# Two decoder layers in one program block, with the first norm's 1/rms applied after the u products

## The chip, the cores and the metric

The kernel runs on one core of a Trainium2 chip. The metric is the device time of one launch in microseconds (us), the median of the runs shown; lower is better. All engine names are those of the profile: PE multiplies matrices, DVE (VectorE), ACT (ScalarE) and POOL (GpSimd) work on elements, SP issues most transfers.

## What is computed

One inference step of a two-layer decoder on 544 tokens (512 of a new sequence, 32 of eight running ones), all in fp32, d_model 1024. What the change touches is the head of a layer and its end:

```python
def layer_step(x, ...):
    h = rmsnorm(x, norm1_g[l])              # x * rsqrt(mean(x*x) + eps) * g
    u, v, o, ig, fg, q, kv, ng, ga, gb = split_cols(h @ w_in[l])
    h_a = mlstm_branch(u, v, o, ig, fg, ...) # causal conv of u, chunked matrix memory
    h_b = nsa(q, kv, gates)                  # compressed + selected + window attention
    merged = sigmoid(ga) * (h_a @ w_branch_a[l]) + sigmoid(gb) * (h_b @ w_branch_b[l])
    x = x + merged @ w_out[l]
    g_ff, u_ff = split(rmsnorm(x, norm2_g[l]) @ w_ffn_up[l])
    x = x + (silu(g_ff) * u_ff) @ w_ffn_down[l]
# two layers, then y = rmsnorm(x, final_norm_g)
```

The caches, states and new rows of both layers are outputs too.

## The kernel before

Activations lie transposed: xT holds x as 8 chunks of 128 channels by 544 tokens; hT (the normed x) has the same shape in the slab. A product with a 128-column piece of a weight is one "group": for each of 8 chunks, two matmuls of 128x128 by 128x272 into a pair of PSUM banks. Four pairs rotate; GROUPS gives the order and the pair of each of the 147 groups of a layer. Weights come as 131 units of 512 KB per layer (UNITS), through a ring of 8 places that SP fills as places come free.

The program is three blocks. The first loads x (8 transfers), the constants and the page table, and sums the squares of x: ACT squares a chunk, DVE adds it to acc. Then a hardware loop over the layers (`nc.Fori(0, DEPTH)`) holds one block in which each engine runs its own list; at its end all layer semaphores are cleared and all engines meet (`nc.all_engine_barrier()`). The last block makes the final norm: a matmul of ones by acc, a root on ACT, a reciprocal on DVE, 8 multiplications and 8 transfers out.

Within a layer, in PE's order: group n1 (ones times acc, which sums the squares over partitions, L799); the four u groups (product, L789); five tm groups (v and the token-major part of kv, L850 and L855); the gates; o; the mLSTM core; q and k; the attention; the branches, out, and the feed-forward in two halves, each ended by eight dn groups (L829). After a dn group DVE adds it to xT (L1924), ACT squares the chunk (L1261) and DVE adds the square to acc (L1548), so that the next layer's n1 finds its sum.

The head of a layer: ACT takes the root of n1 (root, L1276), DVE the reciprocal of all 544 columns (L1567), then makes the 8 chunks of hT by one operation each, `(xT * n1g) * rstd` (L1569), and PE's u groups wait for them chunk by chunk (h_ready). ACT copies each u group into upad with three copies (L1282 to L1285), DVE convolves it (L1581 to L1585), and ACT makes a rounded copy xh of hT (L1289).

SP starts a layer with the small weights' first 40 columns (L645, scales: n1g and others), then unit 0, the rest of the small weights (L654) and the further units (L650). POOL starts a layer with a 2 MB copy of the old window (L668) and four 512 KB loads of the memory state (L672, c0).

In the mLSTM core PE's sample_state(h, a) (L943) adds to the states of the running sequences; each waits until DVE's add_state (L1693) has emptied the bank of the one before it. numerators(h) (L968) waits for DVE's quotients(h-1) (L1674 to L1679). sample_rows on DVE (L1716 to L1723) finishes the 32 sample tokens.

Of the kernel before, what the change touches and what calls it, by code (L numbers as in the profile page):

```python
# [36 lines left out]
P = 128  # L37
# [41 lines left out]
RING = 8  # L79
# [4 lines left out]
GROUPS = ([("n1", 0)] + [("u", m) for m in range(4)] + [("tm", i) for i in range(TT + 1)] + [("if", 0)]  # L84
# [17 lines left out]
QSPLIT, LSPLIT = 4, 12  # L102

# [64 lines left out]
def build_step(nc, xT_in, W_in, small_in, const_in, c0_in, pages_in, table_in, win_in, cwin_in,  # L168
               y_out, fm_out, raw_out, knew_out, tm_out, u_out, pC_out, pn_out, m_out, sC_out, oldwin_out):
    with ExitStack() as ctx:  # L170
        def sb(name, shape, dt=F32):
            return ctx.enter_context(nc.sbuf_tensor(name, shape, dt))

        def sem(name):
            s = ctx.enter_context(nc.semaphore(name))
            layer_sems.append(s)
            return s

        layer_sems = []
# [187 lines left out]
        unit_landed = [sem(f"unit_landed{s}") for s in range(RING)]  # L367
# [4 lines left out]
        page_landed = [sem(f"page_landed{i}") for i in range(4)]  # L372
        raw_ready = sem("raw_ready")
        page_arranged = sem("page_arranged")
        sel_landed = sem("sel_landed")
        win_landed = sem("win_landed")
        c0_landed = [sem(f"c0_landed{h}") for h in range(MH)]
        stored = sem("stored")
        cstored = sem("cstored")
# [15 lines left out]
        u_stored = sem("u_stored")  # L395
        mix_stored = sem("mix_stored")
        raw_stored = sem("raw_stored")
        nsa_stored = sem("nsa_stored")
# [51 lines left out]
        dve_step = sem("dve_step")  # L450
        act_step = sem("act_step")
# [10 lines left out]
        with nc.Block() as block:  # L462
            @block.sync
            def _(sp):
                for k in range(KC):
                    sp.dma_start(xT[:, k, :], xT_in[:, k, :]).then_inc(x_landed[k], 16)
                sp.dma_start(const[:, :], const_in).then_inc(const_landed, 16)
                sp.dma_start(table[:, :], table_in).then_inc(table_landed, 16)

            @block.scalar  # L470
            def _(act):
                for k in range(KC):
                    act.wait_ge(x_landed[k], 16)
                    if k >= 3:
                        act.wait_ge(start_added, k - 2)
                    act.activation(acc[:, :] if k == 0 else sq[:, k % 2, :], xT[:, k, :], ACT.Square).then_inc(start_squared, 1)

            @block.vector
            def _(dve):
                dve.memset(ones[:, :], 1.0)  # L480
                dve.memset(eps[:, :], EPS)
                for k in range(1, KC):
                    dve.wait_ge(start_squared, k + 1)
                    if k >= 2:
                        dve.wait_ge(start_added, k - 1)
                    dve.tensor_tensor(acc[:, :], acc[:, :], sq[:, k % 2, :], ALU.add).then_inc(start_added, 1)
                dve.wait_ge(start_added, KC - 1)

# [97 lines left out]
        def read_out(eng, key):  # L590

            q = GROUP[key]
            eng.wait_ge(pair_free[q % 4], q // 4 + 1)

        def unit_used(eng, n):

            kind, m = UNITS[n]
            if kind == "tm" and m < KC - 1:
                eng.wait_ge(tm_used, m + 1)
            elif kind == "w1":  # L600
                eng.wait_ge(w1_used, m + 1)
            elif UNITS[n] in SPLIT:
                eng.wait_ge(wl_ready, SPLIT[UNITS[n]] + 1)
            else:
                group = ("tm", TT) if kind == "tm" else (kind, m)
                eng.wait_ge(pair_done, GROUP[group] + 1)

        def split_used(eng, n):

            kind, m = SPLITS[n]  # L610
            if kind != "dn":
                eng.wait_ge(pair_done, GROUP[("b", m) if kind == "ab" else SPLITS[n]] + 1)
            else:
                f, u = divmod(m, NFH)
                if u < NFH - 1:
                    eng.wait_ge(dn_used, f * (NFH - 1) + u + 1)
                else:
                    eng.wait_ge(pair_done, GROUP[("dn", f * KC + KC - 1)] + 1)
# [21 lines left out]
        with nc.Fori(0, DEPTH) as layer:  # L640
            with nc.Block() as block:
                @block.sync
                def _(sp):
                    parameters = small_in[bass.ds(layer, 1)].rearrange("l p n -> (l p) n")
                    sp.dma_start(small[:, 0:SMALL_FIRST], parameters[:, 0:SMALL_FIRST]).then_inc(scales_landed, 16)  # L645

                    def unit(n):
                        if n >= RING:
                            unit_used(sp, n - RING)
                        sp.dma_start(ring[:, n % RING, :],  # L650
                                     W_in[bass.ds(layer, 1), n].rearrange("l p n -> (l p) n")).then_inc(unit_landed[n % RING], 16)

                    unit(0)
                    sp.dma_start(small[:, SMALL_FIRST:SMALL_W], parameters[:, SMALL_FIRST:SMALL_W]).then_inc(small_landed, 16)  # L654
                    for n in range(1, len(UNITS)):
                        unit(n)

                    sp.wait_ge(stored, 32)
                    sp.wait_ge(u_stored, 16)
                    sp.wait_ge(mix_stored, 32)  # L660
                    sp.wait_ge(cstored, 16 * MH)
# [1533 lines left out]
```

## Time and profile before

| | |
|---|---|
| three timed runs | 2114.97, 2116.30, 2118.91 us; median 2116.3 us |
| profiled execution | 2117.96 us, its span 2115.6 us |
| PE busy | 2011.2 us, 95% |
| DVE, ACT, POOL busy | 43%, 32%, 4% |
| mean granted PE clock | 0.95 of 2.4 GHz |

The span runs from the first to the last instruction of the core; 2.4 us of the execution's time lie around it. The profiled execution is 1.7 us above the median. A timeline row gives the start, the length, the engine, the line and the operation; what stands in brackets is the engine's idle time just before, and what ended it.

### The profile page before, as it was taken

What the parts mean: (1) busy time and instruction counts of PE and PEld (TensorE: products, weight loads), DVE (VectorE), ACT (ScalarE), POOL (GpSimd) and SP (SyncE); (2) the same over time, 40 slices, a digit from 0 to 9 for tenths busy, and PEclk for the clock granted to TensorE, in tenths of its full rate; (3) what the DMA queues carried; (4) which work ended last, traced back from release to release, by engine and by line L of the source; (5) the groups of instructions that cost most, each with busy time, mean ns of one, the idle gap of its engine ahead of it and who ended that gap; (6) DMA issues with size and microseconds to landing.
All of it is one profiled execution on the core that took longest, in us unless ns stands there. A gap on an engine that the chain in (4) does not pass through costs nothing. (4 is left out here: it accounts for less than half of the span.)

```text
span 2115.6 us, 34303 instructions
## 1 busy us (share of the span) xinstructions
PE 2011.2 (95%) x14138; PEld 1774.4 (84%) x14138; DVE 910.4 (43%) x1594; ACT 667.4 (32%) x1261; POOL 84.2 (4%) x136
## 2 busy tenths in 40 slices
PE   6999999999999999999779999999999999999995
PEld 5586955589999999999756869555899999999995
DVE  4145545633345442444232355565233554424433
ACT  2443256632233221222114322556322332212221
POOL 0001120000000000000000021200000000000000
PEclk9999979979999999999889899799799999999997
DMA  7211450012222222221042023400122222222211
GB/s 273 74 69 52 135 171 1 1 60 90 90 82 89 90 90 82 90 90 51 34 183 110 21 84 121 151 1 11 61 90 91 90 81 91 90 90 83 88 41 43
DMA packets 48114, 176.33 MB, mean 83 GB/s; under 512 B 6506, under 2 KB 6538, under 8 KB 47506
## 3 DMA queue, kind: packets, MB, share of 16 engines
q1 hardware_dynamic: 40754, 144.81, 19.9%
q0 software_dynamic: 7200, 29.27, 4.1%
q8 instruction: 114, 1.87, 0.4%
q14 instruction: 46, 0.38, 0.1%
HBM read 163.47 MB, written 14.71 MB: 84 GB/s over the span
## 5 line engine op out<-in xcount | busy, mean ns | idle before, releaser
L829 PE MATMUL ps<-xh,late_w 128*128 128x272 f32 x3840 | 645.4, 289 | 1.8 <-issue 1.8
L829 PEld LDWEIGHTS ps<-xh,late_w 128*128 128x128 f32 x3840 | 544.9, 190 | 2.5 <-issue 2.3
L1557 DVE TENSOR_TENSOR late_w<-ring,late_w 128x1024 fp32r<-128x1024 f32 x196 | 240.2, 1226 | 653.8 <-ACT late_w L1272 653.8
L1272 ACT CAST late_w<-ring 128x1024 fp32r<-128x1024 f32 x196 | 205.3, 1047 | 727.0 <-PE ps L829 727.0
L829 PE MATMUL ps<-xl,late_w 128*128 128x272 f32 x1920 | 397.6, 289 | 0.0
L829 PEld LDWEIGHTS ps<-xl,late_w 128*128 128x128 f32 x1920 | 303.5, 190 | 0.0
L829 PE MATMUL ps<-ah,late_w 128*128 128x272 f32 x1408 | 234.7, 288 | 0.0
L829 PEld LDWEIGHTS ps<-ah,late_w 128*128 128x128 f32 x1408 | 198.7, 188 | 0.0
L1425 ACT ACTIVATE slab<-ps,stat 128x31 f32<-128x31 f32 (+5 forms) x204 | 84.3, 449 | 118.0 <-DVE stat L1840 118.0
L829 PE MATMUL ps<-mh,late_w 128*128 128x272 f32 x576 | 98.9, 289 | 0.0
L1075 PE MATMUL ps<-slab 64*128 64x512 f32 (+2 forms) x192 | 93.6, 615 | 0.0
L1112 PE MATMUL ps<-slab,vkv 128*64 128x256 f32 x320 | 90.9, 429 | 0.0
L1112 PEld LDWEIGHTS ps<-slab,vkv 128*64 128x64 f32 x320 | 44.0, 151 | 50.8 <-issue 34.3
L829 PEld LDWEIGHTS ps<-mh,late_w 128*128 128x128 f32 x576 | 82.3, 188 | 0.1
L789 PE MATMUL ps<-slab,ring 128*128 128x272 f32 x256 | 64.1, 416 | 18.8 <-DVE slab L1569 18.8
L829 PE MATMUL ps<-al_first,late_w 128*128 128x272 f32 x384 | 79.3, 288 | 0.0
L789 PEld LDWEIGHTS ps<-slab,ring 128*128 128x128 f32 x256 | 51.9, 204 | 31.7 <-issue 20.3
L1435 ACT ACTIVATE slab<-slab,stat 128x128 f32<-128x128 f32 (+4 forms) x140 | 69.0, 555 | 10.7 <-DVE stat L1863 10.4
L1094 PEld LDWEIGHTS ps<-const,slab 128*128 128x128 f32 (+1 forms) x384 | 43.6, 145 | 34.3 <-issue 23.3
L1094 PE MATMUL ps<-const,slab 128*128 128x128 f32 (+1 forms) x384 | 61.1, 300 | 6.0 <-ACT slab L1435 6.0
L829 PE MATMUL ps<-al_rest,late_w 128*128 128x272 f32 x320 | 66.2, 288 | 0.0
L829 PE MATMUL ps<-ml,late_w 128*128 128x272 f32 x320 | 66.1, 288 | 0.0
(324 smaller groups left out, 2688.1 us busy)
## 6 DMA issues: line engine op xcount, KB each, us to landing
ring<-in_W SPq DMA_DIRECT2D x262, 512.0 KB, 3.2
slab<-in_pages POOLq DMA_DIRECT2D x64, 128.0 KB, 2.5
slab<-in_c POOLq DMA_DIRECT2D x8, 512.0 KB, 18.3
out_sC<-slab POOLq DMA_DIRECT2D x8, 512.0 KB, 3.0
slab<-in_win POOLq DMA_DIRECT2D x2, 2048.0 KB, 8.8
out_oldwin<-in_cwin POOLq DMA_DIRECT2D x2, 2016.0 KB, 13.7
xT<-in_xT SPq DMA_DIRECT2D x8, 272.0 KB, 4.3
out_y<-slab SPq DMA_DIRECT2D x8, 272.0 KB, 2.1
```

The lines of the kernel that those rows point to most:

```text
L789: mm = pe.matmul(out[:, a, :], w[:, k, :], src[:, k, a * NHALF:(a + 1) * NHALF], start=(k == 0), stop=(k == kcs - 1))
L829: mm = pe.matmul(out[:, a, :], w[:, k * P:(k + 1) * P], x[:, a * NHALF:(a + 1) * NHALF], start=start, stop=stop)
L1075: mm = pe.matmul(out[:, r], qrT[hd, r0 + r, i * P:(i + 1) * P], kT[hd, brs[0] - 1:brs[-1], 0:(i + 1) * P], start=True, stop=True)
L1094: mm = pe.transpose(ps[0:rows, 5 + x % 2, at:at + P], part, ident)
L1112: mm = pe.matmul(out, vkv[:, j, (br - 1) * P + g * HD:(br - 1) * P + (g + 1) * HD], PT[:, x % 2, 2 * c * P:2 * (c + 1) * P], start=(br == ...
L1272: act.copy(hi, ring[:, u % RING, :]).then_inc(wh_ready, 1)
L1425: ins = act.activation(prob(k)[:, r, :], score(k)[:, r, :], ACT.Exp, bias=stat[:, k % 3, r:r + 1], accum_out=stat[:, 3 + k % 3, r:r + 1] i ...
L1435: ins = act.activation(prob(k)[:, r, :], prob(k)[:, r, :], ACT.Copy, scale=stat[:, 8 + k % 3, r:r + 1])
L1557: dve.tensor_tensor(lo, ring[:, u % RING, :], hi.bitcast(F32), ALU.subtract).then_inc(wl_ready, 1)
```

## The change

Both layers are written out one after the other in one block; the loop, the clearing of semaphores, the barrier and the separate first and last blocks are gone. Semaphores that count per layer go on counting: `on(s, value)` adds the layer's number times the total per layer (TIMES). Semaphores of stores and loads get one copy per layer. Weight units are numbered through both layers (g = 131 * layer + n), so SP goes on filling the ring into the next layer.

The head of a layer is new. DVE makes `hT[k] = xT[k] * n1g` chunk by chunk (gained), at the start of the program as each chunk of x lands, in the second layer behind each of the last eight dn additions. The u groups work on this and wait for it (xg_ready); group n1 comes behind u 0. When the reciprocal is there, DVE takes each u group out of PSUM with a multiplication by rstd (evac_u, three operations, in place of ACT's three copies), and multiplies each chunk of hT by rstd in place once group u 3 has read it (u_read); the tm groups wait for that (h_ready).

```diff
-GROUPS = ([("n1", 0)] + [("u", m) for m in range(4)] + [("tm", i) for i in range(TT + 1)] + [("if", 0)]
+GROUPS = ([("u", 0), ("n1", 0)] + [("u", m) for m in range(1, 4)] + [("tm", i) for i in range(TT + 1)] + [("if", 0)]
...
+                scales(0)
+                for k in range(KC):
+                    sp.dma_start(xT[:, k, :], xT_in[:, k, :]).then_inc(x_landed[k], 16)
+                    if k in (1, 5):
+                        unit(k // 4)
+                parameters(0)
+                for g in range(2, RING):
+                    unit(g)
+                sp.dma_start(const[:, :], const_in).then_inc(const_landed, 16)
+                sp.dma_start(table[:, :], table_in).then_inc(table_landed, 16)
+                for g in range(RING, DEPTH * len(UNITS)):
+                    layer, n = divmod(g, len(UNITS))
+                    if layer + 1 < DEPTH and UNITS[n] == ("fg", NFH):
+                        sp.wait_ge(*on(xl_ready, 2 * KC, layer))
+                        scales(layer + 1)
+                        parameters(layer + 1)
+                    unit(g)
...
-                    norm_sum(("n1", 0), None)
-                        fm("u", m, ready=(h_ready, 0))
+                        product(("u", m), ("u", m), hT, KC, (xg_ready, 0), u_read if m == 3 else None).then_inc(pair_done, 1)
+                        if m == 0:
+                            norm_sum(("n1", 0), None)
...
+                            if i == 0:
+                                pe.wait_ge(*on(h_ready, k + 1))
...
-                    sample_state(1, 1)
                     numerators(3)
+                    sample_state(1, 1)
...
+                def gained(k):
+                    return dve.tensor_scalar(hT[:, k, :], xT[:, k, :], sml("n1g")[:, k:k + 1], None, ALU.mult)
+                for k in range(KC):
+                    dve.wait_ge(x_landed[k], 16)
+                    gained(k).then_inc(xg_ready, 1)
+                    if k >= 1:
+                        dve.wait_ge(start_squared, k + 1)
+                        if k >= 2:
+                            dve.wait_ge(start_added, k - 1)
+                        dve.tensor_tensor(acc[:, :], acc[:, :], sq[:, k % 2, :], ALU.add).then_inc(start_added, 1)
...
+                    for m in range(3):
+                        evac_u(m)
                     for k in range(KC):
-                        dve.scalar_tensor_tensor(out=hT[:, k, :], in0=xT[:, k, :], scalar=sml("n1g")[:, k:k + 1], in1=rstd[:, :],
-                                                 op0=ALU.mult, op1=ALU.mult).then_inc(h_ready, 1)
+                        if k < KC - 1:
+                            dve.wait_ge(*on(u_read, k + 1))
+                        else:
+                            dve.wait_ge(*on(pair_done, GROUP[("u", 3)] + 1))
+                        dve.tensor_tensor(hT[:, k, :], hT[:, k, :], rstd[:, :], ALU.mult).then_inc(h_ready, 1)
+                    evac_u(3)
...
-                    sample_rows()
                     weighted_scores(3)
                     add_state(1, 0)
                     quotients(2)
-                    add_state(1, 1)
+                    sample_rows()
                     split_low(QSPLIT)
...
                     quotients(3)
+                    add_state(1, 1)
...
+                            if name == "dn" and m >= KC and layer + 1 < DEPTH:
+                                if m == KC:
+                                    dve.wait_ge(scales_landed, 32)
+                                read_out(dve, key)
+                                gained(m - KC).then_inc(xg_ready, 1)
...
-            for s in layer_sems:
-                nc.sync.sem_clear(s)
-            nc.all_engine_barrier()
```

POOL's first work in a layer is now the padding of upad; it stores u when all four u groups are out, and then issues the four c0 loads and the copy of the old window, which stood at the layer's start.

PE where the layers meet, before: the last dn matmuls (`ah` and `al_rest` by `late_w`), the loop's branches, and the rows that stand at the head of the list, to which the loop jumps.

```order
L829 MATMUL ps<-ah,late_w 128x272 x2
L641 UNCONDITIONAL_BRANCH
L640 REGISTER_ALU
L640 COMPARE_AND_BRANCH
L1969 UNCONDITIONAL_BRANCH
L1972 MATMUL ps<-acc,ones 128x272 x2
```

```order
L762 UNCONDITIONAL_BRANCH
L799 MATMUL ps<-acc,ones 128x272 x2
L789 MATMUL ps<-slab,ring 128x272 x64
L850 MATMUL ps<-ring,slab 128x512
L855 MATMUL ps<-ring,slab 128x280
```

The n1 matmuls (`acc` by `ones`) stood ahead of all 64 matmuls of the four u groups. The same place now:

```order
L853 MATMUL ps<-al_rest,late_w 128x272 x2
L853 MATMUL ps<-ah,late_w 128x272 x2
L809 MATMUL ps<-slab,ring 128x272 x16
L823 MATMUL ps<-acc,ones 128x272 x2
L809 MATMUL ps<-slab,ring 128x272 x48
L873 MATMUL ps<-ring,slab 128x512
L878 MATMUL ps<-ring,slab 128x280
```

The 16 matmuls of u 0 follow the last dn matmul at once, n1 comes behind them, and no branch is left. DVE where the layers meet, now, from the last dn addition (`xT`) to the first operations of the convolution:

```order
L1990 TENSOR_TENSOR xT<-xT,ps 128x544
L1573 TENSOR_SCALAR slab<-xT,small 128x544
L1600 TENSOR_TENSOR acc<-acc,sq 128x544
L1618 RECIPROCAL rstd<-rstd 128x544
L1623 TENSOR_TENSOR slab<-ps,rstd 128x272
L1624 TENSOR_TENSOR slab<-ps,rstd 128x240
L1626 TENSOR_TENSOR slab<-ps,rstd 128x8x4
...
L1635 TENSOR_TENSOR slab<-slab,rstd 128x544 x8
...
L1647 TENSOR_SCALAR slab<-slab,small 128x512
```

The multiplication by the weight (L1573) stands between the addition to xT and that to acc; the chunks of hT are scaled (L1635) behind the first three u groups. PE in the core, around the second-to-last numerators, before and then now:

```order
L943 MATMUL ps<-slab 128x512
L968 MATMUL ps<-slab 128x129 x10
L943 MATMUL ps<-slab 128x512
L968 MATMUL ps<-slab 128x129 x10
L829 MATMUL ps<-xh,qwk 128x272 x2
```

```order
L966 MATMUL ps<-slab 128x512
L991 MATMUL ps<-slab 128x129 x20
L966 MATMUL ps<-slab 128x512
L853 MATMUL ps<-xh,qwk 128x272 x2
L853 MATMUL ps<-xl,qwk 128x272 x2
```

The state product (128x512) that stood between numerators 2 and 3 now stands behind both.

## Rows read from the trace of the kernel before

**Rows 1.** Page, busy time: engine, us, share of the span, instructions.
```profile
PE 2011.2 (95%) x14138; PEld 1774.4 (84%) x14138; DVE 910.4 (43%) x1594; ACT 667.4 (32%) x1261; POOL 84.2 (4%) x136
```
**Rows 2.** PE's waits: who, for whom: us in total, times, longest us.
```profile
PE ps L789 <- DVE slab L1569: 18.8, 2, 13.4
PE ps L799 <- issue: 12.6, 1, 12.6
```
**Rows 3.** Timeline of the start: start us, us, engine, line, operation, idle before.
```profile
3.81 0.66 ACT L476 ACTIVATE acc<-xT 128x544 f32<-128x544 f32 x1 [1.53 <-DMA xT<-in_xT]
...
12.09 2.15 PE L799 MATMUL ps<-acc,ones 128*128 128x272 f32 x4 [12.09 <-PEq L462]
19.61 11.64 PE L789 MATMUL ps<-slab,ring 128*128 128x272 f32 x37 [5.37 <-DVE slab L1569]
...
30.15 0.39 ACT L1282 COPY slab<-ps 128x272 f32<-128x272 f32 x1 [15.15 <-PE ps L789]
...
51.95 1.02 PE L850 MATMUL ps<-ring,slab 128*128 128x512 f32 x2
```
**Rows 4.** Timeline where the layers meet, by engine PE, DVE and ACT.
```profile
1040.78 0.29 PE L829 MATMUL ps<-ah,late_w 128*128 128x272 f32 x1
1041.11 0.72 DVE L1924 TENSOR_TENSOR xT<-xT,ps 128x544 f32<-128x544 f32 x1 [6.11 <-PE ps L829]
1042.55 0.72 DVE L1548 TENSOR_TENSOR acc<-acc,sq 128x544 f32<-128x544 f32 x1 [0.72 <-ACT sq L1261]
1053.72 2.18 PE L799 MATMUL ps<-acc,ones 128*128 128x272 f32 x4 [12.65 <-issue]
1064.78 3.55 DVE L1567 RECIPROCAL rstd<-rstd 128x544 f32<-128x544 f32 x1 [21.51 <-DMA small<-in_small]
1069.30 10.98 PE L789 MATMUL ps<-slab,ring 128*128 128x272 f32 x38 [13.40 <-DVE slab L1569]
1078.95 0.39 ACT L1282 COPY slab<-ps 128x272 f32<-128x272 f32 x1 [22.29 <-PE ps L789]
```
**Rows 5.** Stretches: length, busy us and counts by engine, PEclk, DMA share, GB/s.
```profile
2.00:12.00 10.00, 0.00 (x0) 0.00 (x0) 5.08 (x7) 5.55 (x10) 0.00 (x0) 1.00 1.00 373
20.00:25.00 5.00, 5.00 (x12) 3.73 (x12) 4.34 (x7) 0.00 (x0) 0.10 (x2) 1.00 1.02 427
25.00:30.00 5.00, 5.00 (x22) 4.08 (x22) 0.00 (x0) 0.00 (x0) 0.57 (x5) 1.00 0.82 333
110.00:480.00 370.00, 350.25 (x2217) 264.19 (x2216) 181.35 (x459) 161.92 (x417) 36.88 (x54) 0.89 0.21 68
480.00:1041.00 561.00, 561.00 (x4472) 560.64 (x4470) 237.26 (x281) 134.84 (x152) 0.00 (x0) 1.00 0.23 79
1160.00:1530.00 370.00, 352.65 (x2204) 264.49 (x2203) 180.31 (x457) 160.70 (x416) 36.70 (x54) 0.88 0.20 67
```
**Rows 6.** One line's durations: ns min/median/max, first and last start, shape.
```profile
L1581 DVE TENSOR_SCALAR slab<-slab,small x8: 546/546/549, 31.0 to 1125.2; 128x512 f32<-128x512 f32 x8
```
**Rows 7.** Timeline of the end, DVE and PE.
```profile
2092.96 0.73 DVE L1548 TENSOR_TENSOR acc<-acc,sq 128x544 f32<-128x544 f32 x1 [0.72 <-ACT sq L1261]
...
2100.82 2.18 PE L1972 MATMUL ps<-acc,ones 128*128 128x272 f32 x4 [9.35 <-PEq L1954]
```
**Rows 8.** PE in the core: state products (L943) and numerators (L968), layers 1 and 2.
```profile
185.66 1.81 PE L943 MATMUL ps<-slab 32*128 32x512 f32 x2 [2.11 <-DVE slab L1693]
187.40 4.67 PE L968 MATMUL ps<-slab 128*128 128x129 f32 x20
...
1240.44 1.12 PE L943 MATMUL ps<-slab 32*128 32x512 f32 x2
1241.96 2.50 PE L968 MATMUL ps<-slab 128*128 128x129 f32 x20 [0.40 <-DVE slab L1679]
```
**Rows 9.** Page, DMA issues, and one line's landing times (SP's weight units, 12 to 20 us).
```profile
slab<-in_c POOLq DMA_DIRECT2D x8, 512.0 KB, 18.3
...
DMA to landing us min/median/max: 3.6/20.6/23.7
```

More of the change, by code:

```diff
@@ L459, in build_step @@
         start_added = ctx.enter_context(nc.semaphore("start_added"))
[L462 to L487, printed above, removed]
+        fin_done = ctx.enter_context(nc.semaphore("fin_done"))
+        fin_root = ctx.enter_context(nc.semaphore("fin_root"))
+        fin_step = ctx.enter_context(nc.semaphore("fin_step"))
+        fin_y = ctx.enter_context(nc.semaphore("fin_y"))
+        fin_stored = ctx.enter_context(nc.semaphore("fin_stored"))
+        yT = slab[:, MIX_AT:MIX_AT + KC * N].rearrange("p (k n) -> p k n", k=KC)
         STEPS = []
@@ L638, in late_events @@
                         yield "group", ("dn", f * KC + c // NFH)
[L640 to L661, printed above, removed]
-                    sp.wait_ge(raw_stored, 32)
-                    sp.wait_ge(nsa_stored, 48)
-                @block.gpsimd
-                def _(pool):
-                    pool.dma_start(oldwin_out[bass.ds(layer, 1)].rearrange("l b n -> (l b) n"),
-                                   cwin_in[bass.ds(layer, 1)].rearrange("l b n -> (l b) n")[:, DECT * 2 * P:PAST * 2 * P]).then_inc(stored, 16)
-                    for h in range(MH):
-                        pool.dma_start(Cst(h).rearrange("p b e -> p (b e)"),
-                                       c0_in[bass.ds(layer, 1), h].rearrange("l p n -> (l p) n")).then_inc(c0_landed[h], 16)
@@ L760, in _ @@
+                    pool.dma_start(tmo[0:NS, TT, :], vkv[0:NS, TT, :]).then_inc(nsa_stored[layer], 16)
+                    pool.wait_ge(stored[layer], 32)
+                    pool.wait_ge(nsa_stored[layer], 48)
+                    pool.wait_ge(win_landed[layer], 16)
+                    pool.wait_ge(sel_landed[layer], 16 * DECB * NPG)
                     pool.dma_reset()
-                @block.tensor
-                def _(pe):
+            @block.tensor
+            def _(pe):
+                for layer in range(DEPTH):
+                    at[0] = layer
@@ L790, in product @@
                                                start=(k == 0), stop=(k == kcs - 1))
+                            if read is not None and k < kcs - 1:
+                                mm.then_inc(read, 1)
                         return mm
@@ L1238, in _, with link @@
                             mm.then_inc(pair_done, 1)
[L1240 to L1248 removed]
+                pe.wait_ge(sq_used, DEPTH * 2 * (KC - 1))
+                for a in range(2):
+                    mm = pe.matmul(ps[:, a, 0:NHALF], ones[:, :], acc[:, a * NHALF:(a + 1) * NHALF], start=True, stop=True)
+                mm.then_inc(fin_done, 1)
+            @block.scalar
+            def _(act):
+                steps = [0]
+                def link(ins):
+                    steps[0] += 1
+                    ins.then_inc(act_step, 1)
+                    act.wait_ge(act_step, steps[0])
+                for k in range(KC):
+                    act.wait_ge(x_landed[k], 16)
+                    if k >= 3:
+                        act.wait_ge(start_added, k - 2)
+                    act.activation(acc[:, :] if k == 0 else sq[:, k % 2, :], xT[:, k, :], ACT.Square).then_inc(start_squared, 1)
+                for layer in range(DEPTH):
+                    at[0] = layer
                     def done(key):
                         q = GROUP[key]
[L1252 removed]
+                        act.wait_ge(*on(pair_done, q + 1))
                         return pair(q), pair_free[q % 4]
```

525 lines of the change are left out of this document (272 added, 253 removed).

## Prediction

> **What bounds the kernel now.** The first view to read is the page's busy time: PE works 95% of the span and the next engine 43% [rows 1]. So the time is PE's work plus the stretches in which PE has none, and only those and PE's clock are worth looking at. The list of PE's waits says where they are [rows 2]: 18.8 us ahead of the u products, in two waits, and 12.6 us ahead of an n1 matmul. The timeline then shows three holes.
>
> At the start PE does nothing until 12.09, sums the squares (n1), and begins u 0 at 19.61 [rows 3]: the whole of x has to be there, squared, rooted and multiplied before the first product.
>
> Where the layers meet, the last dn matmul ends at 1041.07 and u 0 begins at 1069.30 [rows 4]. The reader is to see what fills these 28.2 us: until 1043.3 the last addition to xT and to acc; until 1053.72 the branch, the clearing of semaphores and the barrier; then n1; then the reciprocal, which starts only at 1064.78, because the layer's scales were asked for behind the barrier and land late; then the multiplications.
>
> At the end acc is complete at 2093.69, and the final matmul starts at 2100.82, behind a block boundary [rows 7].
>
> **The start.** Removed: the first block's end, n1 and the reciprocal ahead of u 0. Now u 0 needs unit 0 and, chunk by chunk, x times its weight. Transfers run from 2.0 us on at 373 GB/s [rows 5]. Before, chunk 0 (0.28 MB, so through at 2.75) was used at 3.81 [rows 3], 1.06 us later. Now the scales, two chunks and unit 0 come first, 1.10 MB or 2.9 us: 2.0 + 2.9 + 1.06, and some 0.4 for the scales' issue, an estimate, give 6.4 for the first u matmul. The eighth chunk follows after 3.3 MB, 8.85 us: 12.3. DVE's multiplication takes 0.55 us for 512 columns [rows 6], so 0.58 for 544: 12.9.
>
> Before, u 0 took 10.54 us (19.61 to 30.15), because PE started at its lower level: 12 matmul records in the first five us against 22 in the next five [rows 5]. I take the same 10.5 us: u 0 ends at 16.9. Its last chunk is wanted some 0.9 us earlier, at 16.0, and is there at 12.9, so the sum of squares on ACT and DVE beside it costs nothing; if that cover went, each us of delay past 16.0 would be a us lost. Behind it comes n1. A full-speed group takes 7.3 us ((51.95 - 30.15) / 3 [rows 3]) for 16 matmuls, n1 has two of the same shape: 0.9. The gain is 19.61 - 6.4 - 0.9 = **12.3 us**. Bounds: all 16 matmuls at the lower level take 14.6 instead of 10.5, gain 8.2; without the scales' issue and half of the 1.06, 13.2.
>
> **The meeting of the layers.** Removed: barrier, clearing, wait for the scales, reciprocal and multiplications ahead of u 0. SP's numbering runs on, so the u units are in the ring before dn ends (SP runs eight units ahead, and the last eight dn units are split ahead of use). The scales are reloaded in the feed-forward stage. What is late next? The chunk of x that the last dn group changes: xT at 1041.83 [rows 4], times its weight 0.58 later, 1042.5. u 0 starts at 1041.1 with chunk 0 and reaches chunk 7 after 7 x 0.91 us, at 1047.5. So nothing makes PE wait, by 5 us. DVE's seven other multiplications lie in its idle time between dn groups, 6.11 us each [rows 4]. acc is complete by about 1043.9, long before n1 at 1048.4.
>
> Then the chain that was on the path runs beside u 1 to u 3: n1 until 1049.3, the root, the reciprocal with 3.55 us [rows 4], rstd near 1054. u 3 needs the bank pair of u 0, at 1063.9: DVE empties a group in three pieces, at most three times the 0.72 us that a whole 544-column addition out of PSUM takes [rows 4], so it is free by 1056. The chunks of hT are scaled as u 3 reads them, 0.72 each against 0.91 per step, the last some 0.8 us after u 3. The tm groups' eighth step comes at least 7 x 1.02 us after their first [rows 3]. Covered, by 6 us.
>
> The gain: the hole of 28.2 us; u 0 at full speed, 7.3 instead of 9.65 us (1069.30 to 1078.95), 2.3 more; less 0.9 for n1, which stood in the hole and now stands in the row: **29.6 us**. Below that only with a wait that I don't see, priced as a rival.
>
> **The end.** The final matmul no longer waits for a block: 2093.75 instead of 2100.82, **7.1 us**. Whether it also runs at the higher level (0.9 instead of 2.18 us) is open: after a 2.11 us wait in the core a state product took 1.81 against 1.12 us [rows 8], and here PE waits 2.7 us, so I take no gain; bound 8.4.
>
> **The core.** The state product behind numerators 2 moves behind numerators 3, and DVE's sample_rows behind quotients 2. In layer 1 PE waited 2.11 us for that product's bank, and the product and numerators 3 then ran slow, 1.81 and 4.67 us [rows 8]; in layer 2 the product, 1.12 us, filled most of the gap before numerators 3, which then waited only 0.40 and took 2.50. Without the product there, the gap stays and the product comes on top: a loss of 1.1 us in a layer like the second, 2.2 for both. In a layer like the first, DVE reaches quotients 2 without the sample rows: up to 2.1 for the wait and 2.9 for the slow run, a gain of at most 5.0 less 1.1. I take **0**, bounds -2.2 and +3.9.
>
> **The rest.** ACT loses twelve small copies per layer and DVE gets twelve multiplications in their place; neither bounds. The convolution of u 0 and u 1 moves behind u 3, but its results are wanted only by ACT behind the first tm groups. POOL's padding waits for the last dn group and is wanted behind u 3. c0 and the old window come some 30 us later within the layer; the states are first read in the core. The unrolled list runs the same PE instructions less the branches.
>
> **The sum.** 12.3 + 29.6 + 7.1 + 0 = 49.0. The profiled execution of 2117.96 becomes 2069.0; it lies 1.66 above the median, so 2116.3 - 49.0 = **2067.3 us**.
>
> **Rivals.**
>
> *A transfer stalls tm.* Unit tm 7 goes into the ring place of u 3, so it is asked for when u 3 ends, and POOL's 4 MB (c0, old window), moved behind u, start a little later. When weights and that load were queued together, units took a median of 20.6 us to land and c0 18.3 [rows 9]. tm 7 is wanted 7.1 us after its issue or later: a stall of up to 13.5 us per layer, 27 in all, 2094 us. Against it: the unit is asked for ahead of them, and alone it needs 0.52 MB / 373 GB/s = 1.4 us and a landing (3.6 at the least). 5%.
>
> The Trainium skill, "DMA: Bandwidth & Descriptors", section "Issuing engines are not separate DMA queues", says that transfers issued by different engines run on the same 16 DMA engines and interleave; by it the move of POOL's loads could slow SP's unit as here. The trace agrees as to layer starts [rows 9]; which is ahead here no run shows yet.
>
> *The start gives nothing*, because unit 0 lands late among 0.5 to 4 MB of others or DVE is held up: 49.0 - 12.3 = 36.7, 2079.6 us. For it: SP's first transfers keep all engines full (DMA share 1.00) [rows 5]. Against: order of issue. 6%.
>
> *The layers don't join.* If a u unit is only asked for at the end of dn, PE waits one landing, 3.6 to 23.7 us [rows 9]: 2071 to 2091. For it, the ring's order is a matter of eight waits; against, all of them lie before the last dn group. 3%.
>
> *Slower, by the clock.* In the mixed stage of a layer (core and attention) the granted clock is 0.89 and 0.88, against 1.00 in 561 us without a gap [rows 5]. Those 740 us lose 7.4 us for each 0.01 of mean clock. If the moved product's gap makes PE fall to the lower level there more often, the gain is gone below 0.885 - 49/740 = 0.82; at 0.80 the time would be 2130. For it: the slow row behind the 2.11 us wait [rows 8]. Against: layer 2 has gaps at other places and the same mean. 2%.
>
> **How the numbers follow.** The forecast has 84%. Around it, clock luck moves 3.7 us, the difference of 0.01 over 370 us between the layers [rows 5]. The best case, 13.2 + 29.6 + 8.4 + 3.9 + 3.7 = 58.8, gives 2057.5; the worst, 8.2 + 29.6 + 7.1 - 2.2 - 3.7 = 39.0, gives 2077.3. The range 2058 to 2080 also holds the start's rival. A measurement of this kernel tells 0.2%, 4 us, from no change. Faster 0.97, within it 0.01, slower 0.02.
>
> **What would show it.** After: u 0 as the first PE work, near 6.4; no PE idle time between the last dn and u 0; n1 in under 1 us; tm within 31 us of the last dn; the final matmul within 0.2 us of the last addition to acc. A wait of tm (the 128x512 line) for a transfer would speak for the first rival, a u 0 later than 10 us for the second, a mean clock below 0.85 between the tm groups and the branches for the last. I am wrong outright if PE's busy time grows by what the holes lose.

## The result and the profile after

| | before | after |
|---|---|---|
| median of four timed runs | 2115.64 us | 2064.97 us (2058.51 to 2068.96) |
| ratio after/before, 95% interval | | 0.9753 (0.9728 to 0.9777) |
| profiled execution, its span | 2117.96, 2115.6 us | 2068.96, 2067.3 us |
| mean granted PE clock | 0.950 | 0.958 |

Forecast 2067.3 us (2058 to 2080). The two profiled executions differ by 49.0 us, the sum that was forecast; the medians differ by 50.7 (the changed kernel's profiled execution is the longest of its four). That a sum comes out right doesn't show that its terms are, so the trace is cut at the places of the terms. The end of dn is the start plus the length of its last matmul row, "tm" is the first 128x512 matmul of a layer.

| stretch | before | after | gain | forecast |
|---|---|---|---|---|
| span start to tm, layer 1 | 51.95 | 39.92 | 12.03 | 12.3 |
| tm to end of dn, layer 1 | 989.12 | 991.12 | -2.00 | 0 (core and clock) |
| end of dn to tm, layer 2 | 59.68 | 30.08 | 29.60 | 29.6 |
| tm to end of dn, layer 2 | 990.72 | 990.12 | 0.60 | 0 (core and clock) |
| end of dn to span's end | 24.13 | 16.06 | 8.07 | 7.1 |
| outside the span | 2.36 | 1.66 | 0.70 | 0 |

The busy row of the page, to be set beside [rows 1]:

```profile
PE 2005.3 (97%) x14138; PEld 1771.2 (86%) x14138; DVE 924.0 (45%) x1634; ACT 663.3 (32%) x1237; POOL 84.0 (4%) x136
```

PE's two waits with the largest totals (who, for whom: us in total, times, longest), to be set beside [rows 2]:

```profile
PE ps L1178 <- ACT slab L1518: 7.5, 6, 2.1
PE ps L809 <- DMA ring<-in_W: 7.4, 1, 7.4
```

The waits of 18.8 and 12.6 us are gone; the one wait left at the u products (L809) is for weight unit 0, at the start. PE's timeline of the start, which answers to [rows 3], and the eighth multiplication of x on DVE:

```profile
7.39 9.78 PE L809 MATMUL ps<-slab,ring 128*128 128x272 f32 x32 [7.39 <-DMA ring<-in_W]
17.01 1.08 PE L823 MATMUL ps<-acc,ones 128*128 128x272 f32 x4
17.93 22.16 PE L809 MATMUL ps<-slab,ring 128*128 128x272 f32 x96
39.92 1.02 PE L873 MATMUL ps<-ring,slab 128*128 128x512 f32 x2
...
13.59 0.49 DVE L1573 TENSOR_SCALAR slab<-xT,small 128x544 f32<-128x544 f32 x1
```

u 0 is PE's first work, n1 stands in the row behind it and costs 0.92 us (17.01 to 17.93). The meeting of the layers, PE and DVE, answers to [rows 4]:

```profile
1030.62 0.42 PE L853 MATMUL ps<-ah,late_w 128*128 128x272 f32 x2
1030.88 7.50 PE L809 MATMUL ps<-slab,ring 128*128 128x272 f32 x32
1038.21 1.08 PE L823 MATMUL ps<-acc,ones 128*128 128x272 f32 x4
1039.12 22.16 PE L809 MATMUL ps<-slab,ring 128*128 128x272 f32 x96
1061.12 1.02 PE L873 MATMUL ps<-ring,slab 128*128 128x512 f32 x2
...
1031.83 0.50 DVE L1573 TENSOR_SCALAR slab<-xT,small 128x544 f32<-128x544 f32 x1
1040.07 3.55 DVE L1618 RECIPROCAL rstd<-rstd 128x544 f32<-128x544 f32 x1 [6.83 <-ACT rstd L1313]
1044.33 0.18 DVE L1626 TENSOR_TENSOR slab<-ps,rstd 128x32 f32<-128x32 f32 x1
1061.32 0.72 DVE L1635 TENSOR_TENSOR slab<-slab,rstd 128x544 f32<-128x544 f32 x1 [0.19 <-PE ps L809]
```

No PE row has a bracket: there is no idle time from dn to tm. The reciprocal, which PE waited for, now lies in the middle of the 22.16 us of u 1 to u 3. The end, to be set beside [rows 7]:

```profile
2052.72 0.72 DVE L1600 TENSOR_TENSOR acc<-acc,sq 128x544 f32<-128x544 f32 x1 [0.72 <-ACT sq L1298]
...
2053.50 1.18 PE L1265 MATMUL ps<-acc,ones 128*128 128x272 f32 x4 [2.26 <-DVE acc L1600]
```

### The profile page after: what moved, and what is told of

It reads as the page before. It is cut to its first block, busy times and chain, and to the rows that moved or that the text cites. A ratio compares the mean times of both kernels' runs of the same rounds, so it can differ in the third digit from the quotient of the medians.

```text
span 2067.3 us, 33438 instructions
## 1 busy us (share of the span) xinstructions
PE 2005.3 (97%) x14138; PEld 1771.2 (86%) x14138; DVE 924.0 (45%) x1634; ACT 663.3 (32%) x1237; POOL 84.0 (4%) x136
## 4 chain that ended last, share of the span: by engine, by line
PE 91%; DVE 4%; ACT 3%; issue 1%; DMA 1%; POOLq 0%; DVEq 0%; POOL 0%; SPq 0%
PE ps L853 62%; PE ps L1098 4%; PE ps L1135 4%; PE ps L809 3%; PE ps L873 3%; PE ps L1117 3%; PE ps L878 2%; PE ps L1198 2%; PE ps L1183 1%; PE ps L978 1%; PE ps L887 1%; PE ps L966 1%; PE ps L991 1%; PE ps L1096 1%; PE ps L1132 1%
## 5 line engine op out<-in xcount | busy, mean ns | idle before, releaser
L809 PE MATMUL ps<-slab,ring 128*128 128x272 f32 x256 | 61.6, 403 | 7.4 <-DMA ring<-in_W 7.4
L873 PE MATMUL ps<-ring,slab 128*128 128x512 f32 x128 | 65.4, 592 | 0.0
```

What stands on the lines that cost most here:

```text
L809: mm = pe.matmul(out[:, a, :], w[:, k, :], src[:, k, a * NHALF:(a + 1) * NHALF], start=(k == 0), stop=(k == kcs - 1))
L873: pe.matmul(ps[:, s, :], x, w[:, 0:512], start=(k == 0), stop=(k == KC - 1))
```

## Experiments

The theory: PE bounds, the gain is the three holes, and each part of the change is needed to close them. The rivals: one part alone brings the gain; the order of the transfers, not the norm, brings it; the chain that was moved beside the u products is not really hidden; the core's new order is a gain or a loss of its own.

### Each part alone

One block, with the norm ahead of u (e_merged_only):

```diff
-GROUPS = ([("u", 0), ("n1", 0)] + [("u", m) for m in range(1, 4)] + ...
+GROUPS = ([("n1", 0)] + [("u", m) for m in range(4)] + ...
-    product(("u", m), ("u", m), hT, KC, (xg_ready, 0), ...)...
+    product(("u", m), ("u", m), hT, KC, (h_ready, 0))...
```

> The changed kernel with one part undone: both layers stand in one block, but group n1 stands ahead of the u groups again, DVE makes hT by (x * weight) * 1/rms behind the reciprocal, and ACT copies u out. My theory: the two parts need each other. Without the deferred norm the joined layers lose the barrier only. End: 8 us as in the changed kernel. Meeting: the hole shrinks from 28.2 to the chain last addition (2.9 us behind the last dn), n1 0.9 to 2.2, root 1.0, reciprocal 3.55, one multiplication 0.72: 9 to 10.5 us, gain 18. Start: x has landed at about 13.6 instead of 12.1, then the same 7.5 us, u 0 at 21: a loss of 1.4. Sum 25, about 2091 us (2086 to 2096). Rival, the parts simply add and the barrier was the meeting's cost: the u groups start within 3 us of the last dn and the time is within 5 us of the changed kernel's 2065.

Measured 2085.91 us, ratio 0.9864 (0.9836 to 0.9893), just below the 2086 to 2096 that were expected. By stretches of the profiled execution: start -2.88 (tm at 54.83; -1.4 was expected), meeting 19.08 (40.60 us from dn to tm; 18), end 7.43 (8), together 23.6. That execution is 32.8 us shorter than the profiled one of before; 8.5 us of it lie in the layers between (4.34 and 4.13), where the granted clock was 0.90 in both mixed stages (0.89 and 0.88 before), and 0.7 outside the span. What stands in the hole:

```profile
1041.96 2.03 PE L821 MATMUL ps<-acc,ones 128*128 128x272 f32 x4 [2.35 <-DVE acc L1597]
1049.30 10.90 PE L807 MATMUL ps<-slab,ring 128*128 128x272 f32 x40 [5.31 <-DVE slab L1619]
```

9.69 us of hole are left (1039.61 to 1049.30), all of it the norm's chain, and u 0 behind it runs below full speed (40 matmul records in 10.90 us at a granted clock of 0.86, where the changed kernel has 32 in 7.50).

Loop and barrier, with the deferred norm (e_defer_only); the head of the layer is the changed kernel's, SP's list and the blocks are those of before:

```diff
-    norm_sum(("n1", 0), None)
-    for m in range(4): fm("u", m, ready=(h_ready, 0))
+    for m in range(4):
+        product(("u", m), ("u", m), hT, KC, (xg_ready, 0), ...)
+        if m == 0: norm_sum(("n1", 0), None)
```

> The kernel before with one part alone: loop, barrier and separate first and last blocks stay, but the first norm's 1/rms is applied behind the u products. My theory: at the head of a layer the scales, which are asked for behind the barrier, are then what PE waits for. In layer 2 the reciprocal stood at 1064.78 because of them; a multiplication of 0.5 us instead of reciprocal and longer multiplication, u 0 near 1065.5 instead of 1069.3, less 1.0 for n1 in the row: 2.8 us. Layer 1 the same or less (reciprocal at 15.10, u 0 at 19.61, the first unit asked for at 12.73): 0 to 3. Sum 3 to 6 us, about 2111 (2108 to 2114). With the joined block alone at 25, the two make 30 of the 50 us, and 20 come only with both. Rival, the norm's chain was the main cost: over 15 us faster.

Measured 2116.96 us, ratio 1.0005 (0.9984 to 1.0026): nothing. The forecast of 3 to 6 us missed a wait. The waits in the window where the layers meet (1050 to 1085 us):

```profile
PEld ps L791 <- DMA ring<-in_W: 26.6, 1, 26.6
PE ps L791 <- DVE slab L1563: 26.3, 1, 26.3
```

The timeline there, DVE and PE, and below it PE in layer 1:

```profile
1065.19 3.39 DVE L1563 TENSOR_SCALAR slab<-xT,small 128x544 f32<-128x544 f32 x8 [21.57 <-DMA small<-in_small]
1067.76 10.49 PE L791 MATMUL ps<-slab,ring 128*128 128x272 f32 x32 [26.34 <-DVE slab L1563]
...
30.16 22.27 PE L791 MATMUL ps<-slab,ring 128*128 128x272 f32 x96 [2.21 <-DMA ring<-in_W]
```

The list names DVE for PE's wait, but DVE's first chunk is done at 1065.6; it is the weight load (PEld) that waits for unit 0, until 1067.75. Who asked for what, POOL and SP, and unit 0's time to landing:

```profile
1051.82 0.59 POOL L670 DMA_DIRECT2D out_oldwin<-in_cwin  x1 [743.52 <-issue]
1052.49 2.30 POOL L674 DMA_DIRECT2D slab<-in_c  x4
1054.99 0.38 SPq L652 DMA_DIRECT2D ring<-in_W  x1
...
DMA to landing us min/median/max: 12.7/12.7/12.7
```

In layer 1 unit 1 is late too (2.21 us). The norm's chain is gone and the transfer behind the barrier is what ends last. POOL's 4 MB, which stand at the layer's head in this kernel as in the one before, were asked for ahead of that unit; a kernel with the barrier kept and those loads moved was not run, so how much of the zero is the barrier's and how much is theirs stays open.

By stretches one block alone is worth 23.6 us, the deferred norm alone -0.3 (start -0.32, meeting 0.10, end -0.10), both together 49.7 (12.03 + 29.60 + 8.07): 26 us come only when nothing else is left that PE must wait for.

### The hidden chain

Idle reciprocals on DVE's chain between the real one and the first multiplication of u (two in e_cover7, six in e_cover21):

```diff
+    for _ in range(2):
+        link(dve.reciprocal(sq[:, 0, :], rstd[:, :]))
     for m in range(3):
         evac_u(m)
```

> The changed kernel with two further reciprocals of 3.55 us (into a scratch tile that nothing reads) between the reciprocal and the first multiplication of u by 1/rms: 7.1 us more on DVE's chain in each layer. The prediction hid this chain beside u 1 to u 3. In the changed kernel u 0 is out of its banks at 1044.5, and u 3 wants them at about 1053.8: 9.3 us of slack in layer 2, and 23.3 against 32.6 in layer 1. Theory: nothing moves, tm starts within 0.3 us of 39.92 and 1061.12 (relative to the last dn, 30.25). Rival, the chain still sets the start of tm through another wait: both 7 us later.

Measured 2064.75 us; dn to tm in layer 2 30.08, as without them, and n1 to tm in layer 1 22.92 against 22.91. u 1 to u 3 there stand in one row, as in the changed kernel:

```profile
19.83 22.16 PE L809 MATMUL ps<-slab,ring 128*128 128x272 f32 x96
```

tm of layer 1 itself starts at 41.83, because unit 0 landed at 8.76 and u 0 took longer, ahead of the chain in question.

> The same with six further reciprocals, 21.3 us more on DVE's chain in each layer. Theory: the slack of 9.3 us is used up, u 3 starts 12.0 us late, and after such a wait PE runs below its higher level for some us (u 0 behind the 13.40 us wait of the kernel before took 9.65 instead of 7.3): 12.0 to 14.5 per layer, 24 to 29 in all. Rival, PE is held elsewhere than at u 3: a wait at another line, or more than 32 us in all.

Measured 2092.23 us; n1 to tm in layer 1 37.16 (14.25 more), dn to tm in layer 2 44.48 (14.40 more). The place is u 3 in layer 1:

```profile
45.18 9.40 PE L809 MATMUL ps<-slab,ring 128*128 128x272 f32 x32 [12.19 <-issue]
```

12.19 us of wait ahead of u 3, and u 3 takes some 2 us longer (45.18 to 54.41, 9.23 against the 7.3 that the prediction took for a group; the granted clock was 0.80 there). So the chain is hidden by 9.3 us, at the place that the prediction named (u 3 wants u 0's banks), and once the cover is gone each us costs one, with 2 more for the clock.

### The transfers at the head

POOL's 4 MB (memory state, old window) back at the layer's head (e_loads_early):

```diff
                     if layer:
                         pool.wait_ge(*on(pair_done, 0))
+                    for h in range(MH):
+                        pool.dma_start(Cst(h)..., c0_in[...]).then_inc(c0_landed[layer][h], 16)
+                    pool.dma_start(oldwin_out[...], cwin_in[...]).then_inc(stored[layer], 16)
```

> The changed kernel with POOL's four loads of the memory state and its copy of the old window at the head of the layer, where they stood. The prediction let them move at no cost, and did not count their move as a gain. Theory: in layer 1 their 4 MB share the engines with x and unit 0. At 370 GB/s they alone need 11 us, so the last chunk of x is multiplied at up to 24 instead of 13.59, u 0 starts at 8 to 11 instead of 7.39, and tm 3 to 9 us later than 39.92; in layer 2 the ring is full when they start, and nothing moves. The move is then part of the start's gain, which the prediction gave to the deferred norm alone. Rival: the engines serve SP's earlier requests first and tm starts within 1 us of 39.92.

Measured 2074.44 us. Layer 2 doesn't move (30.08). In layer 1 tm starts at 53.67, 13.75 us later and later than in the kernel before; 3 to 9 were expected. Two PE rows and the multiplication between them:

```profile
9.53 5.65 PE L809 MATMUL ps<-slab,ring 128*128 128x272 f32 x16 [9.53 <-DMA ring<-in_W]
23.98 6.94 PE L809 MATMUL ps<-slab,ring 128*128 128x272 f32 x16 [8.80 <-DVE slab L1573]
...
23.43 0.50 DVE L1573 TENSOR_SCALAR slab<-xT,small 128x544 f32<-128x544 f32 x1 [8.57 <-DMA xT<-in_xT]
```

In the middle of u 0 PE waits 8.80 us for a chunk of x, the fifth, which SP asked for at 3.7. Just ahead of it, at 3.67, POOL had asked for the copy of the old window. The copy's row, its time to landing, and the chunk's:

```profile
3.67 0.58 POOL L691 DMA_DIRECT2D out_oldwin<-in_cwin  x1
DMA to landing us min/median/max: 19.4/19.4/19.4
DMA to landing us min/median/max: 19.7/19.7/19.7
```

The copy landed at 23.1, some 9.8 us behind the last of the four loads (13.2), and the chunk right behind it, at 23.4. The expectation had given all 4 MB one rate and 11 us; the copy's 2 MB alone took nearly that. The start's gain belongs to the order of the transfers as much as to the deferred norm: 12.03 with both, -2.88 without the deferred norm, -1.72 without this order (51.95 less 53.67).

The same loads in between, issued when u 2 is out of its banks, ahead of the request for unit tm 7 (e_loads_mid):

```diff
-                    for m in range(4):
+                    for m in range(3):
                         read_out(pool, ("u", m))
+                    ... the four loads and the copy of the old window ...
+                    read_out(pool, ("u", 3))
```

> The changed kernel with POOL's four loads of the memory state and its copy of the old window issued once u 2 is out of its banks (33.6 and 1054.8 in the changed kernel), some 6 us ahead of the request for unit tm 7 (40.12 and 1061.32) and not 3 us behind it. This tells apart what the rival on a stalled tm rests on: whether the request's place in time saves tm, or the engines' room. Theory, what is asked for first takes the engines: of the 4 MB, 11 us at 370 GB/s, some 5 us are left when unit tm 7 is asked for, so it lands 8 to 15 us after its issue and not 3.6; tm's eighth step comes 9.3 us after the first matmul of tm, so tm waits 0 to 6 us per layer for the transfer. Rival: the unit lands within 5 us all the same, and tm never waits.

Measured 2081.45 us. PE's waits in tm (L874) in this kernel:

```profile
PE ps L874 <- DMA ring<-in_W: 11.2, 2, 5.9
```

The landing time of the unit that SP asked for at 41.67, from the view of SP's line:

```profile
DMA to landing us min/median/max: 15.1/15.1/15.1
```

PE's timeline at tm's eighth step in layer 1:

```profile
56.80 2.08 PE L874 MATMUL ps<-ring,slab 128*128 128x512 f32 x2 [5.85 <-DMA ring<-in_W]
```

In the changed kernel the same unit lands 3.6 us after its issue (3.7 in layer 2), with POOL's loads asked for 3 us behind it, not 6 us ahead:

```profile
DMA to landing us min/median/max: 3.6/3.6/3.6
```

In e_loads_mid the last of the four loads landed at 44.7, the copy of the old window at 55.7 and the unit, asked for 3.5 us behind that copy, at 56.8. The engines were not full meanwhile (length, busy us and counts by engine, PEclk, DMA share, GB/s):

```profile
44.67:55.72 11.05, 6.28 (x20) 3.31 (x18) 5.35 (x13) 0.00 (x0) 0.00 (x0) 0.97 0.49 194
```

By that DMA share of 0.49 the engines had room, so of the two that this run was to tell apart it speaks for the request's place in time. This is the rival of the stalled tm, at 5.9 and 5.3 us of wait, and with the slow matmuls behind it (2.08 us for the first pair, otherwise 1.02) 7 to 8 us per layer from tm to the core's first matmul that spreads the gates (`ps<-acc,const`, 4x512): 107.21 and 106.79 us against 99.99 and 98.68.

The Trainium skill, "DMA: Bandwidth & Descriptors", section "Issuing engines are not separate DMA queues", says that transfers interleave on the same engines whichever engine started them. The traces agree that SP's transfers and POOL's are not independent (15.1 against 3.6 us for one unit).

### The core's order

The order of before in the changed kernel, PE's product and DVE's two pieces, the sample rows and the addition of that state (e_old_core):

```diff
+                    sample_state(1, 1)
                     numerators(3)
-                    sample_state(1, 1)
...
+                    sample_rows()
                     weighted_scores(3)
                     add_state(1, 0)
                     quotients(2)
-                    sample_rows()
+                    add_state(1, 1)
...
                     quotients(3)
-                    add_state(1, 1)
```

> The changed kernel with the core's order as it was: PE's state product (1,1) ahead of numerators 3, DVE's sample rows ahead of the weighted scores 3 and the addition of that state ahead of the low parts. The prediction took 0 for this move, with bounds of -2.2 and +3.9 us. Theory: from the start of tm to the first q group the two orders differ by less than 2 us per layer, most of it clock; PE waits some 2 us ahead of the state product in one or both layers instead of 2.19 and 1.45 ahead of numerators 3. Rival, the move explains the 1.84 us that layer 1 lost between tm and the last dn: with the old order layer 1 is 1.5 to 2.5 us shorter.

Measured 2070.47 us, tm to dn 990.66 and 991.37. From tm to the first q group it took 143.40 and 140.32 us, the changed kernel 140.48 and 143.23: 2.9 us apart in each layer where under 2 was expected, but with opposite signs, so that the sums agree. The place is short enough to be read by itself: from the start of numerators 2 to the first q matmul. Before 10.67 and 6.21 us; with the old order in the changed kernel 6.21 and 9.59; with the new order, in the changed kernel, 9.81 and 7.43. PE there, layers 1 and 2 of the changed kernel, then layer 2 of the old order:

```profile
175.28 4.14 PE L991 MATMUL ps<-slab 128*128 128x129 f32 x20 [2.19 <-DVE slab L1745]
179.35 1.12 PE L966 MATMUL ps<-slab 32*128 32x512 f32 x2
...
1200.87 2.50 PE L991 MATMUL ps<-slab 128*128 128x129 f32 x20 [1.45 <-DVE slab L1745]
1203.30 1.12 PE L966 MATMUL ps<-slab 32*128 32x512 f32 x2
```
```profile
1196.71 1.22 PE L966 MATMUL ps<-slab 32*128 32x512 f32 x2 [2.12 <-DVE slab L1759]
1197.98 3.94 PE L991 MATMUL ps<-slab 128*128 128x129 f32 x20
```

Both orders have a good and a bad case, and either case came in either layer. The old order gives 6.2 or 9.6 to 10.8 us, the new one 7.4 or 9.8 to 11.2, over six and sixteen passes; the means are 8.3 and 8.9. The means mix the cases (three of six and seven of sixteen were good ones): in the good case the old order is 1.2 us shorter, in the bad case the two overlap. The rival that the move explains layer 1's loss of 2.00 us falls, as far as one execution of each tells: layer 1 with the old order was 990.66, 0.46 us shorter and not 1.5 to 2.5.

### A combination, and the spread

The changed kernel with unit 0 asked for ahead of x and PE's product ahead of numerators 3, DVE as changed (e_both_small, and in more rounds e_both_five; beside them the changed kernel itself, e_after_again and e_after_five):

```diff
                 scales(0)
+                unit(0)
                 for k in range(KC):
                     sp.dma_start(xT[:, k, :], xT_in[:, k, :]).then_inc(x_landed[k], 16)
-                    if k in (1, 5):
-                        unit(k // 4)
+                    if k == 5:
+                        unit(1)
...
+                    sample_state(1, 1)
                     numerators(3)
-                    sample_state(1, 1)
```

> The changed kernel with two small edits, each read at its own place. First: weight unit 0 is asked for right behind the scales, ahead of x, since u 0 waited for it until 7.39 although chunk 0 was multiplied at 4.75. By the theory that the first transfers share the engines and land in their order, chunk 0 lands about 1.4 us later and unit 0 about 1 us earlier: u 0 near 6.3, gain 1.0; tm starts 1 us earlier. Rival: it lands no earlier because issue and landing are not in step (u 0 at 7.0 to 7.6). Second: PE makes the state product (1,1) ahead of numerators 3 again, while DVE keeps the new order. By the theory that it fills the gap of 2.19 and 1.45 us there, each layer's core is shorter by 1.05. Sum 3 us, near 2062. Rival for the second: the product's bank is not free at that time and the gap moves ahead of it.

> The changed kernel once more, unchanged, as the measure for the three others on this chip. Expected 2058 to 2069 us, ratio 0.973 to 0.978, with the time going with the mean granted clock (0.962 at the short end, 0.958 at the long one).

> The changed kernel with unit 0 asked for ahead of x and the state product (1,1) ahead of numerators 3 once more, in more rounds. From the first look: tm starts 1 to 3 us earlier than in the changed kernel (38.8 against 39.9 to 41.8), and the stretch from numerators 2 to the first q group takes 6.3 and 8.2 us where the changed kernel took 7.4 to 9.8. Expected 2060 us, 2 to 5 below the changed kernel on this chip. Rival: the difference lies inside the spread that the clock makes, and the two medians are within 2 us.

> The changed kernel, unchanged, beside it in as many rounds: 2063 to 2066 us, ratio 0.974 to 0.978.

Measured on one chip 2060.54 (0.9734, 0.9707 to 0.9760) against 2063.02 (0.9761, 0.9708 to 0.9814), on another 2059.67 (0.9721, 0.9702 to 0.9741) against 2061.97 (0.9739, 0.9721 to 0.9757). The wide interval of 0.9761 comes from one execution of four that took 2078.44 us; 2061.97 lies a little below the 2063 to 2066 that were expected. Both times the combination is 2.3 to 2.5 us lower, and both times the intervals overlap: by the totals it isn't told apart from the changed kernel. At their places the edits show. PE's first row of the first run, then the core in layer 2 of the second:

```profile
6.99 9.08 PE L810 MATMUL ps<-slab,ring 128*128 128x272 f32 x32 [6.99 <-DVE slab L1574]
```
```profile
1186.70 1.12 PE L967 MATMUL ps<-slab 32*128 32x512 f32 x2
1188.22 2.50 PE L992 MATMUL ps<-slab 128*128 128x129 f32 x20 [0.41 <-DVE slab L1746]
```

u 0 starts at 6.99 and 6.50 and waits for x, no longer for unit 0; 6.3 was expected, and the rival had 7.0 to 7.6 with unit 0 still late. With the changed start it began at 7.39 to 8.84. tm starts at 38.82 and 38.25, against 39.92, 40.88 and 40.01 in the changed kernel's three traces. Numerators 2 to q takes 6.3 or 8.2 us, mean 7.3 over four passes, 1.7 less than the new order's. The best core of the sixteen passes with the new order took 38.07 us from the first spread of the gates to q, the best of the four here 36.96: the 1.1 us of the product, which fills the gap as the prediction said it did before.

## Why the prediction was right, and where only its sum was

**The bound.** Right: what left the holes left the time, and PE's busy time fell by 5.9 us instead of growing (the mean granted clock rose from 0.950 to 0.958).

**The start, 12.03 for 12.3.** Right by two errors that cancel. The step "2.0 + 2.9 + 1.06, and some 0.4" gave 6.4 for u 0; it was 7.39, and 7.45 to 8.84 in six other traces with the same start. The order of landing held (chunk 1 was multiplied at 5.30, unit 0 let u 0 start at 7.39, chunk 2 was multiplied at 8.06). The rate didn't: the 373 GB/s are a mean over ten us, and the first of these moved less in the kernel before already, and less again now. Length, busy us and counts by engine, PEclk, DMA share, GB/s, one row of before and three of after:

```profile
2.00:5.00 3.00, 0.00 (x0) 0.00 (x0) 0.00 (x0) 1.45 (x3) 0.00 (x0) 1.00 0.96 303
...
2.00:5.00 3.00, 0.00 (x0) 0.00 (x0) 0.51 (x1) 0.81 (x2) 0.00 (x0) 1.00 0.85 254
0.00:5.00 5.00, 0.00 (x0) 0.00 (x0) 0.68 (x3) 1.94 (x2) 0.20 (x4) 1.00 0.52 154
5.00:10.00 5.00, 2.61 (x6) 2.02 (x7) 2.98 (x6) 2.39 (x4) 0.00 (x0) 1.00 1.00 367
```

So 1.10 MB are through at about 5.9 (0.77 MB by 5.0, the rest at 367 GB/s), an estimate; with the 1.06 of the sum that is 7.0, and the last 0.4 us to 7.39 stay open. u 0 then took 9.62 us, not 10.5. The prediction gave PE's lower level as the reason for a slow u 0; the granted clock is 1.00 there, in [rows 5] and from 7.39 to 17.01 now, so the granted clock doesn't show it and the reason stays open. The eighth chunk was multiplied at 14.1, not 12.9, still 2 us ahead of its use. And the part named the first block's end, n1 and the reciprocal as what goes; the line on POOL's loads, "c0 and the old window come some 30 us later", was right as a cost, but their move is what keeps the start's 12 us (13.75 lost without it).

**The meeting, 29.60 for 29.6.** Right step by step: no idle time ahead of u 0, n1 0.91, rstd 12.6 us behind the end of dn (1043.62 less 1031.04; the prediction had 1054 less 1041.1), u 0 out of its banks 9.3 us ahead of u 3 (forecast some 8), the last chunk of hT scaled 0.8 us behind u 3's last matmul, as forecast. The two runs with longer chains priced the cover.

**The end, 8.07 for 7.1.** The hole went as forecast; the final matmul also ran at the higher level (1.18 us at a granted clock of 1.00 against 2.18), which the prediction had left out on the ground of a slow state product behind a 2.11 us wait. PE waited 2.26 us here, not the 2.7 of the prediction. Over the eleven traces of joined kernels, each with a wait of 2.26 us, the matmul took 1.18 or 1.19 eight times and 1.79, 1.89 and 2.18 once each. The usual case is thus 7.1 and 1.0 on top, with 7.1 as the worse case. The bound of 8.4 was too high by 0.3: it set the 0.9 by which n1 delays the group behind it against the 2.18 of a whole row, and a whole row at the higher level takes 1.08 to 1.18.

**The core and the clock, -1.4 for 0.** The bounds held, and their reading did: a layer like the second of before lost 1.22 (1.1 forecast), one like the first gained 0.86. The other -1.0 is the sum of larger pieces: 1.6 gained from tm to the core (nearly all in layer 2, granted clock 0.98 before and 1.00 now), 1.7 lost in layer 1 from the core's start to numerators 2, and 0.9 lost from q to dn. The second piece before and then now (length, PE's busy us and count, PEclk, DMA share, GB/s):

```profile
152.05:181.05 29.00, 28.11 (x218) 1.00 0.02 7
139.91:170.59 30.68, 29.79 (x219) 0.94 0.02 7
```

PE's idle time is the same there (0.89 us) and the clock is not; why it fell, and what the last 0.9 us are, no run shows. The stretch from tm to dn took 983 to 991 us in the traces of joined kernels (e_loads_mid left out, for its stall): 4 us to either side, for each layer, where the prediction allowed 3.7 for both.

**The sum.** That 49.0 came out to the digit is luck. Against the forecast the start gave 0.3 less, the end 1.0 more and the layers between 1.4 less, and 0.7 came from outside the span, which the prediction did not count. Nor is this execution typical of the layers between: over ten traces of joined kernels the two stretches from tm to dn average 988.7 and 986.9 us, over the two with the barrier 989.1 and 990.7.

**The rivals.** The stalled tm is real at another place of the loads (15 us over both layers, by the stretches), and that it didn't come here was a matter of the 3 us between two requests. The others didn't come.

## What to carry to other kernels

Before closing a hole, list everything that ends in it: with the norm's chain alone moved, the transfer behind the barrier took its place; with the barrier alone removed, the norm's chain kept a third of it. A step that is hidden should be given its slack in us and the row that sets it; two runs with idle work on either side of that number tell whether it is right. In these runs a request landed late when another engine had asked for bulk transfers ahead of it (right behind the old window's copy a chunk of x landed at 23.4 us, in the changed kernel the same chunk landed at 9.4), so a request that is on the path goes ahead of them.

## What the runs showed of the hardware

The same wait can be followed by either level of PE's clock: the final matmul behind 2.26 us of idle time took 1.18 us at a granted clock of 1.00, 2.18 at 0.50, and 1.79 and 1.89 between them. A 512 KB unit landed in 3.6 us when 4 MB were asked for 3 us behind it and in 15.1 us when they were asked for 6 us ahead, with a DMA share of 0.49 over 11 of these us. The copy of the old window, 2 MB, landed 9.8 and 11.0 us behind the last of four loads asked for just ahead of it, and what was asked for behind it landed right after it. The kernel before ran from 2107.73 to 2123.31 us in thirteen executions on one chip, so differences of 2 or 3 us here are to be read at their place in the trace, not in the total.
